# One step earlier: the last MLP chunks, the statistics behind the second chunk, and 32 stationary columns for the step sizes

## The reference, cut to what matters

```python
h = h + sqrelu_mlp(rms_norm(h, mlp_norm[layer]), mlp_w1[layer], mlp_w2[layer])
...
kv = rms_norm(h, kv_norm) @ w_kv            # after MLP 0: shared keys and values
k = rms_norm(k.reshape(B, S, DIFF_HEADS, 2, DIFF_DH), k_norm)
...
u = rms_norm_2(h, norm_mix[i])              # after MLP 1: the second block
proj = u @ w_in[i]                          # convolution, z, xbc, dt, q, k, v, gates
dt = jax.nn.softplus(dt_raw.astype(jnp.float32) + dt_bias.astype(jnp.float32))
```

## Time and profile before

| | |
|---|---|
| median of 3 runs | 1583.28 us (1581.59 to 1583.49) |
| the profiled execution, its own time | 1579.73 us |
| span of the trace | 1577.9 us |
| mean granted TensorE clock | 0.959 of full |
| PE busy | 1426.4 us (90%) |
| DVE busy | 1035.2 us (66%) |
| ACT busy | 889.3 us (56%) |
| POOL busy | 329.9 us (21%) |

### The profile page before, as it was taken

The page is one execution under the profiler, slowest core; times in us unless marked ns, Lnnn a source line. Parts: engine busy times, 40 slices in busy tenths (PEclk is TensorE's granted clock), DMA queues, the critical chain, the costliest instruction groups (busy, mean ns, idle before and its releaser), DMA issues. The chain is left out here.

```text
span 1577.9 us, 30012 instructions
## 1 busy us (share of the span) xinstructions
PE 1426.4 (90%) x11488; PEld 1294.0 (82%) x11488; DVE 1035.2 (66%) x1661; ACT 889.3 (56%) x1693; POOL 329.9 (21%) x334
## 2 busy tenths in 40 slices
PE   7987999989879999989877779898898979799999
PEld 6876999988757999989877667777777779599998
DVE  6794755566656666647999755568576666375555
ACT  4434655456556555548988655454565466365553
POOL 2000411132004111126878100004000004051111
PEclk9998999999987999979999989999999989999999
DMA  7320555545713555534434322234434335055552
GB/s 305 132 107 29 189 200 197 186 161 132 216 54 107 194 203 191 187 107 171 151 136 157 128 86 102 86 107 161 137 126 149 124 134 188 27 188 194 204 189 81
DMA packets 35603, 233.72 MB, mean 148 GB/s; under 512 B 4000, under 2 KB 7072, under 8 KB 8352
## 3 DMA queue, kind: packets, MB, share of 16 engines
q1 hardware_dynamic: 31104, 223.75, 39.8%
q10 hardware_dynamic: 3216, 4.19, 1.7%
q0 software_dynamic: 1168, 4.20, 0.9%
HBM read 227.93 MB, written 4.19 MB: 147 GB/s over the span
## 5 line engine op out<-in xcount | busy, mean ns | idle before, releaser
L1484 DVE TENSOR_TENSOR w_lo<-raw,w_hi 128x1024 bf16<-128x1024 f32 x420 | 536.1, 1277 | 242.4 <-ACT w_hi L942 239.0
L942 ACT CAST w_hi<-raw 128x1024 fp32r<-128x1024 f32 x420 | 438.7, 1047 | 351.7 <-PE ps L406 179.3
L396 PE MATMUL ps<-xa_both,w_hi 128*128 128x256 f32 x1808 | 464.9, 297 | 32.6 <-ACT w_hi L942 11.1
L397 PE MATMUL ps<-xa_both,w_hi 128*128 128x256 f32 x1808 | 439.7, 283 | 0.0
L396 PEld LDWEIGHTS ps<-xa_both,w_hi 128*128 128x128 f32 x1808 | 350.9, 194 | 44.1 <-issue 25.0
L397 PEld LDWEIGHTS ps<-xa_both,w_hi 128*128 128x128 f32 x1808 | 351.8, 195 | 0.6
L406 PE MATMUL ps<-xa_bf,w_lo 128*128 128x256 bf16 x1808 | 240.2, 277 | 21.4 <-DVE w_lo L1484 21.4
L406 PEld LDWEIGHTS ps<-xa_bf,w_lo 128*128 128x128 bf16 x1808 | 160.7, 99 | 49.3 <-DVE w_lo L1484 24.8
L440 PE MATMUL ps<-xb_both,w_hi 128*128 128x256 f32 x768 | 188.4, 288 | 0.0
L441 PE MATMUL ps<-xb_both,w_hi 128*128 128x256 f32 x768 | 180.0, 277 | 0.0
L396 PE MATMUL ps<-xb_both,w_hi 128*128 128x256 f32 x576 | 149.7, 299 | 13.5 <-DVE xb_both L1497 7.8
(11 more groups left out here) (288 smaller groups left out, 1932.9 us busy)
## 6 DMA issues: line engine op xcount, KB each, us to landing
raw<-weights SPq DMA_DIRECT2D x210, 1024.0 KB, 4.8
band<-arena ACTq DMA_DIRECT2D x1, 3072.0 KB, 35.4
arena<-band POOLq DMA_DIRECT2D x8, 256.0 KB, 3.2
arena<-gla_masks SPq DMA_DIRECT2D x1, 1088.0 KB, 15.6
H<-x_t SPq DMA_DIRECT2D x2, 512.0 KB, 4.8
arena<-mem_t POOLq DMA_DIRECT2D x1, 1024.0 KB, 5.2
arena<-band POOLq DMA_DIRECT2D x8, 128.0 KB, 2.6
out_t<-H ACTq DMA_DIRECT2D x8, 128.0 KB, 2.0
```

The lines of the kernel that those rows point to most:

```text
L396: mm(ps[:, bank, 0:T], w_hi[:, s, k], X.hi[:, k], start=k == 0, stop=False)
L397: mm(ps[:, bank, 0:T], w_hi[:, s, k], X.lo[:, k], start=False, stop=False)
L942: nc.scalar.copy(w_hi[:, j % HI_SLOTS].rearrange("p k n -> p (k n)"), raw[:, j // 2 % RING, j % 2]).then_inc(hi_done, 1)
L1484: TT(w_lo[:, j % HI_SLOTS].rearrange("p k n -> p (k n)"), raw[:, j // 2 % RING, j % 2], w_hi[:, j % HI_SLOTS].rearrange("p k n -> p (k n)" ...
```

## The change

Four edits:

1. In the last group of MLP 0 and MLP 1, DVE does `final(p)` ahead of the `cut_lo` of the same step, where it came behind it (the third MLP has no `cut_lo` left there).
2. ACT's `final` makes both hi tiles of a pair and then both bf tiles, where it made hi, bf, hi, bf.
3. `stats` is issued on PE after the second chunk of the DK and of the CONV stage, where it was after the first.
4. The step sizes are computed with the 32 columns of `dt_hi`, `dt_lo` as stationary operand and the 256 tokens as moving one, 24 matmuls into 32 partitions; DVE multiplies by `rstd` into `dt_rows` (a slice of `sqtmp`), PE transposes the two halves back after the chunk C+2, and DVE adds `dt_bias`. ACT casts C+3, C+4 ahead of `rms`, C+5 behind it, and the small operations on DVE come one chunk later.

```diff
-                    if n == 0:
+                    if n == 1:
                         stats(2, True, True)
...
             chunk(C_CONV, C_CONV, XA, XA_MIX)
+            chunk(C_CONV + 1, C_CONV + 1, XA, None)
             stats(4, True, True)
             pe.wait_ge(split_hi, 2)
             pe.wait_ge(split_lo, 2)
+            for k in range(KC):
+                mm(ps[0:SSD_HEADS, 4, 0:T], dt_hi[:, k], XA.hi[:, k], start=k == 0, stop=False)
+                mm(ps[0:SSD_HEADS, 4, 0:T], dt_hi[:, k], XA.lo[:, k], start=False, stop=False)
+            for k in range(KC):
+                last = mm(ps[0:SSD_HEADS, 4, 0:T], dt_lo[:, k], XA.bf[:, k], start=False, stop=k == KC - 1)
+            last.then_inc(sa["dtf"], 1)
+            chunk(C_CONV + 2, C_CONV + 2, XA, None)
+            pe.wait_ge(sa["dts"], 1)
             for t in range(NT):
-                at = slice(t * P, (t + 1) * P)
-                to = ps[:, 4, t * SSD_HEADS:(t + 1) * SSD_HEADS]
-                for k in range(KC):
-                    mm(to, XA.hi[:, k, at], dt_hi[:, k], start=k == 0, stop=False)
-                    mm(to, XA.lo[:, k, at], dt_hi[:, k], start=False, stop=False)
-                for k in range(KC):
-                    last = mm(to, XA.bf[:, k, at], dt_lo[:, k], start=False, stop=k == KC - 1)
+                last = nc.tensor.transpose(ps[:, 5, t * SSD_HEADS:(t + 1) * SSD_HEADS], dt_rows[:, t * P:(t + 1) * P],
+                                           ident[0:SSD_HEADS, 0:SSD_HEADS])
             last.then_inc(sa["dt"], 1)
-            chunks(C_CONV + 1, 7, XA, None)
+            chunks(C_CONV + 3, 5, XA, None)
...
                 def final(pair):
                     act.wait_ge(bank_free, c0 + 56 + 2 * pair + 2)
                     for n in (2 * pair, 2 * pair + 1):
-                        operand(X, build, n, H[:, n], pcol(gain, n))
+                        A(X.hi[:, n], H[:, n], ACT.Copy, scale=pcol(gain, n)).then_inc(X.hi_done, 1)
+                    for n in (2 * pair, 2 * pair + 1):
+                        A(X.bf[:, n], H[:, n], ACT.Copy, scale=pcol(gain, n)).then_inc(X.bf_done, 1)
...
-            cut_hi(C_CONV + AHEAD, C_CONV + AHEAD)
+            for n in range(2):
+                cut_hi(C_CONV + n + AHEAD, C_CONV + n + AHEAD)
             rms(4, rstd, rtok)
+            cut_hi(C_CONV + 2 + AHEAD, C_CONV + 2 + AHEAD)
...
                     for j in range(8):
+                        if last and j >= 5:
+                            final(j - 5)
                         cut_lo(c + 8 + j + AHEAD, o + j + AHEAD)
                         if j == 0:
                             operand_lo(XB, n0 + 8, 7, m_sq[:, 1])
-                        if last and j >= 5:
-                            final(j - 5)
                         if last and X is not None and j >= 6:
                             final_lo(j - 6)
...
                 if n == 0:
-
+                    dve.wait_ge(sa["dtf"], 1)
+                    TT(dt_rows, ps[0:SSD_HEADS, 4, 0:T], rstd[0:SSD_HEADS], ALU.mult).then_inc(sa["dts"], 1)
+                if n == 1:
                     dve.wait_ge(sa["dt"], 1)
                     for t in range(NT):
                         at = slice(t * SSD_HEADS, (t + 1) * SSD_HEADS)
-                        ins = STT(s_small[:, 0, at], ps[:, 4, at], rtok[:, t:t + 1], pcol("dt_bias", 0, SSD_HEADS), ALU.mult, ALU.add)
+                        ins = TT(s_small[:, 0, at], ps[:, 5, at], pcol("dt_bias", 0, SSD_HEADS), ALU.add)
                     ins.then_inc(sa["dtx"], 1)
-                if n == 1:
+                if n == 2:
                     dve.wait_ge(sa["dta"], 1)
```

More of the change, by code:

```diff
@@ L204, in program @@
         dt_hi, dt_lo = [x[:].rearrange("p (k h) -> p k h", k=KC) for x in (small_hi, small_lo)]
+        dt_rows = sqtmp[0:SSD_HEADS]
         cut = Cut(decayed_at)
@@ L301, in program @@
         ca = {n: sem("c_" + n) for n in ("sig", "in", "tap", "prod", "add", "mean", "xc", "sq", "var", "r", "norm", "silu")}
-        sa = {n: sem("s_" + n) for n in ("tap", "silu", "z", "dt", "dtx", "dta", "dte", "da", "cs", "bias", "x", "xd", "cb", "cbs", "c", "e",
+        sa = {n: sem("s_" + n) for n in ("tap", "silu", "z", "dtf", "dts", "dt", "dtx", "dta", "dte", "da", "cs", "bias", "x", "xd", "cb", "cbs", "c", "e",
                                          "sc", "y", "yd", "sq", "n", "r", "on", "eb")}
@@ L1196, in _ @@
             for n in range(16):
-                if n:
+                if n > 2:
                     cut_hi(C_CONV + n + AHEAD, C_CONV + n + AHEAD)
```

## The result

| | before | changed |
|---|---|---|
| median | 1583.28 us (1579.67 to 1587.40, 5 runs) | 1571.26 us (1568.96 to 1573.21, 5 runs) |
| profiled execution, its own time | 1579.73 us | 1571.05 us |
| span | 1577.9 us | 1569.2 us |

The ratio is 0.9927, 95% interval 0.9905 to 0.9948: 12.0 us by the medians, between 8.2 and 15.0 us. The forecast was 1571.5 us, 11.8 us less.

What follows compares the result with a forecast made beforehand. TensorE, busy 1426.4 of 1577.9 us, was taken as the bound. Gains of 2.2 us at DK and 10.2 at CONV, less 0.6, made 11.8: from 1583.3 to 1571.5 us, range 1565.5 to 1577.5.

Steps and rivals of the forecast that it cites:

- The pause: End of an MLP: pair 2 is added before D7 ends, so PE's idle of 4.44 us before the next chunk goes.
- The first chunk's end: Behind MLP 1: the next stage's first chunk ends at 689.7 to 690.5 against 694.7, 4.6 us earlier at each boundary.
- lo of pair 0 until 681.7 (1.23 for two): VectorE at the end of MLP 1: two lo tiles take 1.23 us, after which pair 2 is added.
- The clock: Behind each MLP boundary: PE's clock falls to half once; 3.0 to 3.4 us of dense work loses 1.5 to 1.7.
- rival B: Clock never falls at the boundaries: DK gains 3.9, CONV 12.3, together 16.2 us, giving 1567.1; chance 0.20.
- strict reading: At the boundaries: pauses under 1 us with matmuls between are no idle window, so the clock stays at 1.00.
- The bounds without a fall: Upper bounds of the gain if the clock stays full: 3.9 us at DK, 12.3 at CONV.
- DK: Up to the third chunk behind MLP 0: gain 2.2 us, including a new 2.3 us wait; bounds -1.2 to 3.9.
- rival C: At DK the 2.3 us wait brings a second clock fall; about 7 us gained in all, 1576.3; chance 0.25.
- CONV: Up to the start of C+3 behind MLP 1: 700.9 against 711.1, gain 10.2 us; bounds 7.5 to 12.3.
- The sum: Whole kernel: 2.2 at DK plus 10.2 at CONV is 12.4 us, less 0.6 for the DK wait: 11.8.

Runs made afterwards that it cites:

- e5: Changed kernel with 19 extra matmuls nobody reads filling PE's pauses in the first chunk of DK and of CONV: 1568.5 us, ratio 0.9893.
- e10: Changed kernel with the step sizes back as 48 matmuls with 32 moving columns, behind the second chunk and statistics: 1574.2 us, ratio 0.9930.
- e2: Kernel before with only the statistics moved behind the second chunk at DK and CONV: 1581.7 us, ratio 0.9980.
- e1: Kernel before with only the residual additions ahead of the weight split and hi tiles ahead of bf tiles: 1577.8 us, ratio 0.9958.
- e7: Changed kernel with the statistics back behind the first chunk at DK only: 1573.6 us, ratio 0.9923.
- e3: Kernel before with only the step sizes as 24 wide matmuls, statistics still behind the first chunk: 1578.3 us, ratio 0.9954.
- e9: Changed kernel with the statistics back behind the first chunk at both DK and CONV: 1571.7 us, ratio 0.9903.
- e4: Changed kernel with each `head_sums` at DK one chunk later: 1568.1 us, ratio 0.9888.
- e6: Changed kernel with both the extra matmuls in PE's pauses and each `head_sums` at DK one chunk later: 1567.6 us, ratio 0.9883.
- e8: Changed kernel with ScalarE's `final` back in the order hi, bf, hi, bf: 1571.6 us, ratio 0.9910.

## Why the prediction was right, and where it was not

**The pause.** Right. The addition of pair 2 came at 683.71, 0.5 us before the D7 w_lo matmuls began (forecast 0.7), and PE did not wait for it.

**The first chunk's end.** Too early by 0.9 us: forecast 7.7 behind D7's w_lo start (690.1), measured 8.56 at both boundaries. Little of it is VectorE. "lo of pair 0 until 681.7 (1.23 for two)" was too short, with 1.7 for two, and pair 2 came 0.3 us late for it; but the last lo tile was there at 6.3, inside the forecast's 5.9 to 6.5, and the stretch 2.85 for four was right. The rest is the clock, which fell before the chunk had ended: in e5, at full clock throughout, the chunk ended at 7.5. So half clock cost 1.0 us in the first chunk alone, and the forecast had 0.4 for it.

**The clock.** It fell once at each boundary, as forecast, and rival B (1567.1) is wrong for this kernel. So is the strict reading of "idle window" in the Trainium skill (TensorE: Matmul & The Clock Gate, "What's actually happening"): no piece of idle was longer than 0.73 us, and in e10 the clock fell with PE never idle. But one fall was sized at 3.0 to 3.4 us of dense work, and 0.50 lasted 6.8 us at both, twice as long. The second chunk and its share took 4.24 us at CONV (12.80 - 8.56) and 4.39 at DK, where 3.6 was forecast. e5 gives the whole price: 2.6 us at DK and 2.4 at CONV. By its own terms the sum holds 1.3 at DK (0.4 in the 690.1, 0.9 on the second chunk) and 1.9 at CONV. This is the largest term that was mis-sized. (The bounds without a fall, 3.9 and 12.3, don't follow from these terms, which give 3.5 and 12.1.)

**DK.** The wait was 2.17 for 2.3. The gain was 0.6 us (17.0 to 16.4) for 2.2; 0.9 of the missing 1.6 is the chunk's end and 0.8 the second chunk's clock. It lies within the stated bounds of -1.2 to 3.9. The fall behind the wait (rival C) did not come in the changed kernel; it came in e2. But even the 0.6 did not last. From D7 of MLP 0 to D7 of MLP 1 the kernel before took 338.2 us and the changed one 338.3: a stretch at 0.50 now lies at 405.7 to 409.1, where before the clock was 1.00. From the third chunk to D7 of MLP 1 the changed kernel, e1 and e7 to e10, which have that stretch, took 321.9 or 322.0 us, and before, e3 and e5, which don't, 321.1 or 321.2. What brings it was not tested. So at DK the change gave nothing that lasted, and neither did e1, e7 or e9; e4 and e5 did, with 335.3 and 334.9 us from D7 to D7.

**CONV.** Step sizes 2.9 us for 2.72, C+2 2.98 for 2.72, transposes 0.25 for 0.3, no wait at C+6. The gain was 8.9 us for 10.2. The sum put 7.3 us of step sizes down to half clock without asking what kept it there. Two pairs of runs answer that: with the 48 narrow matmuls the clock stayed at 0.50 to 708.0 (before) or fell to it (e10), and with the 24 wide ones in their place it returned at 697.4 (e3) or stayed at 1.00 (changed).

**The sum.** 0.6 + 8.9 = 9.5 us at the boundaries for 12.4. In the profiled pair 1.7 us were lost before DK and 0.6 between the boundaries, and 1.5 gained behind C+3 (866.8 to 865.3 us to the end): 8.7. The 1.7 is scatter: up to the last chunks of MLP 0 no run changes the code, and the twelve profiles reach D7 of MLP 0 anywhere from 343.9 to 348.7 us. The 1.5 hangs on where one stretch at 0.50 lies, ahead of a wait of PE for ScalarE or behind it:

```profile
PE ps L702 <- ACT arena L1237: 1.7, 1, 1.7
```

(PE's waits in the changed kernel: us in total, times, longest.) The same wait before:

```profile
PE ps L697 <- ACT arena L1228: 3.4, 1, 3.4
```

The windows of the stretch, first in the changed kernel and then before (columns as in the windows above):

```profile
866.50:869.90 3.40, 3.40 (x9) 2.69 (x9) 3.26 (x7) 0.63 (x2) 0.00 (x0) 0.50 0.42 111
885.50:888.90 3.40, 2.90 (x7) 2.37 (x8) 1.96 (x3) 3.38 (x7) 0.00 (x0) 0.50 0.85 308
```

The wait ended 174.9 us behind C+3 in both. In the changed kernel the stretch lies ahead of it and only shortens the wait, which costs nothing; before, it lay at the wait's end (886.0) and slowed the work behind it. PE's next long wait (9.2 us in both) ended 199.6 us behind C+3 in the changed kernel and 201.0 before. The other profiles fall in the same two groups: 201.0 to 201.6 where a stretch lies behind the wait (e1, e5, e6), 199.6 to 199.8 where it doesn't. So this 1.5 us is not the edits' work: e5, which has them all, gave it back.

The medians differ by 12.0, 2.5 more than the boundaries show. So the direction, the size of the gain at CONV and the single fall of the clock were foreseen, but that 11.8 was hit so closely is luck: the sum was 2.9 us too large at the boundaries, and what the medians have beyond them made up for it. What that is stays open in part. One piece is the sample: the profiled execution of the kernel before (1579.7) is among its fastest, with a median of 1585.4 over the 24 runs beside e1 to e4. e7, e8 and e9, equal at the boundaries to within 0.2 us, have ratios from 0.9903 to 0.9923.

**Which edit.** Alone the edits gave at CONV 3.6 (1, 2), 3.2 (3) and 5.3 us (4), 12.0 together, and 8.9 in one kernel. Edits 3 and 4 cure the same thing, small matmuls at half clock. Taken away one at a time, edit 4 is worth 2.2, edit 3 and edit 2 nothing. Edit 1 was not taken away from the changed kernel; e8 suggests that e1's 3.6 us are its own, but what it is worth beside edits 3 and 4 was not measured.

## What to carry to other kernels

Price a pause of TensorE with what runs at half clock behind it, and test that by filling the pause with matmuls nobody reads: if the successor comes earlier, the clock was the cost. When a step is moved behind another chunk, look at what used to be covered by that chunk and now follows directly; here `head_sums` one chunk later was worth 2.6 us, and the move itself nothing. Edits that remove the same loss don't add, so judge each by taking it out of the final kernel. And where a gain is read at one place, read it again at the next landmark: the 0.6 us at DK was gone 50 us later.

## What was not expected of the hardware

- 48 matmuls with 32 moving columns, back to back for 4 us with PE busy throughout, were followed by a granted clock of 0.50 (e10 at 702.4 us, and e2 at 710.1); the same work as 24 matmuls with 256 moving columns was not (changed kernel, 1.00 from 695.9 to 703.6), and the clock returned from 0.50 during it (e3, 697.4).
- A wait of 2.2 us with full-width work around it left the clock at 1.00 in the changed kernel and in e5, e8 and e10; in e2 it was followed by 0.50 from 365.4 to 368.8. What decides between them was not tested.
- Two lo tiles on VectorE took 1.70 and 1.72 us in the changed kernel and 1.22 and 1.23 before, four took 2.85 in both. POOL was at work for most of each of these stretches, so what sets the price is not shown.
- A stretch of 3.4 us at 0.50 cost about 1.5 us where the work behind a wait ran in it, and nothing where it lay ahead of the wait.
